# Front of a decoder block in two halves of the model width, with angles and three casts moved to GpSimd

## The chip, the cores and the metric

One core of a Trainium2 chip. The metric is the device time of one execution in microseconds (us). The kernel uses TensorE (PE; its weight loads are listed as PEld), VectorE (DVE), ScalarE (ACT), GpSimd (POOL) and SyncE (SP), which issues nearly all DMAs. Each engine runs its own list of instructions in order, and engines wait for each other on semaphores.

## The reference

x is 1024 tokens by a model width of 1024, one batch, one layer, all in float32:

```python
mod = (silu(c) @ w_ada + b_ada)          # 1024 -> 6 * 1024
sh1, sc1, g1, sh2, sc2, g2 = split(mod, 6)
h = rms_norm(x, norm1_g) * (1 + sc1) + sh1
q, k, v, u = split(h @ w_in)             # 512, 128, 128, 512 columns
q = rope(rms_norm(q, q_norm_g), cos, sin)       # cos, sin of positions * inv_freq
k = rope(rms_norm(k, k_norm_g), cos, sin)
attn = sliding_window_attention(q, k, v, sinks) # window 128, 8 heads on 2
pooled = trailing_means(u, (2, 4, 8, 16)) - u   # four groups of 128 channels
pool_out = (pooled @ pool_w) * pool_scale
x = x + g1 * (concat(attn, pool_out) @ w_o)
h2 = rms_norm(x, norm2_g) * (1 + sc2) + sh2
out = x + g2 * (square(relu(h2 @ w_mlp_in)) @ w_mlp_out)
```

The first rows of a trailing mean divide by the number of tokens there are (1, 2, ... up to the window).

## The kernel before, in words

**Precision.** Every operand of a projection is split in a high part (a cast to fp32r) and a low part (the float32 value less the high part). A product is three matmuls: high by high, low by high and high by low. The cast is ScalarE's work (names with `hi_`), the subtraction VectorE's (names with `lo_`).

**Tiles.** The tokens are eight tiles of 128 (t = 0 to 7). The model width is KD = 8 blocks of 128; NK = 4 is half of it.

**Modulation.** sh1 and sc1 are sums over the 1024 rows of w_ada. A row belongs to a partition and one of eight pieces, so VectorE multiplies a loaded piece (128 x 1024) by one column of silu(c) and adds it to an accumulator (`add_piece`, L1193 to L1199), eight pieces for sh1 in `acc`, then eight for sc1 in `acc_sc` (which is `squares`). PE then sums over the partitions with column sums: 128 columns of the accumulator as weights, a column of ones as the moving operand (`column_sum`, L2047). VectorE adds the biases and gains and has b1 (shift) and a1 (scale), one value for each of the 1024 columns of the width (L1251, `scale_1` at L1255).

**h.** x is loaded by tiles (`load_x`), squared and scaled by its root mean square (`square_x`, `root` on GpSimd, `scale_x`), turned by PE (`turn_x`) and multiplied by a1 and shifted by b1 as it is read from PSUM: the first half of the width by VectorE (`make_h`), the second by ScalarE (`make_h_half`). `hi_h` and `lo_h` split it. Both halves of a tile need all of a1 and b1 for their columns.

**Loads.** `stream` (L219) is the order in which SP loads the pieces: 8 of sh1, 8 of sc1, 4 of w_in for u (`wu`), 8 of w_in for q, k and v (`wqkv`), then the pieces of the later modulations, w_o, x and w1. Up to EARLY they go around twelve buffers (4 in `raw`, 8 in `slots`); a load waits for what was twelve places ahead to be used up (`freed`). x of tiles 0 and 1 goes behind the eighth piece (L540).

**The front on PE.** The order is written out by hand (L2177 to L2278): turn the bias and position rows; eight column sums of sh1; `turn_x(0)`, `turn_x(1)`; filler matmuls (`keep_clock`, which write nothing that is used) between the last pieces of sc1; column sums of sc1 in two halves; fillers; then tile 0's u projection over all eight blocks (`project_u_first`), its q, k and v (`project_qkv_first`), tile 1's u, `pool_windows(0)`, `turn_x(2)`, tile 1's q, `pool_out(0)`, tile 1's k and v, `turn_qk(0)`, tile 2's u. A column sum, a filler or any other matmul with float32 operands is two instructions in the trace, a transpose is one.

**Angles and sines.** VectorE computes positions times inverse frequencies and brings them into the range of the sine (`angles`, L1201), between `sum_qk(0)` and `norm_k(0)`. ScalarE takes the sines behind `scale_x(2)` (`sines`, L872).

**Pooling.** The trailing means are matmuls of u with four band matrices that GpSimd makes (`band`, L1853 to L1872). The first rows have other divisors, so GpSimd makes the bands for tile 0 first and rebuilds their first columns after tile 0's windows (L1927 to L1937).

**Later modulations.** sh2, sc2 and g1 are summed piece by piece in `acc`, one after the other, between the work of the tiles (`add_job_pieces`, with `first_pieces`, `between_pieces` and `late_pieces` giving the pieces of each tile, and JOB_LOADS the loads). Their sums are turned at t = 3 and t = 5.

Of the kernel before, what the change touches and what calls it, by code (L numbers as in the profile page):

```python
# [16 lines left out]
P = 128  # L17
# [36 lines left out]
def build(nc, x, c, positions, w_ada, b_ada, norm1_g, w_in, q_norm_g, k_norm_g, attn_sinks,  # L54
# [30 lines left out]
    with ExitStack() as ctx:  # L85
# [38 lines left out]
        mr = small[:, 90:98]  # L124

# [109 lines left out]
        JOB_LOADS = (4, 4, 4, 3, 4, 4, 1, 0)  # L235
        adaln_jobs = ("sh2", "sc2", "g1", "g2")
        mod_of = {"sh1": SH1, "sc1": SC1, "g1": G1, "sh2": SH2, "sc2": SC2, "g2": G2}
# [34 lines left out]
        a1_ready = sem("a1_ready")  # L272
        wu_hi, wu_lo = sem("wu_hi"), sem("wu_lo")
        wqkv_hi, wqkv_lo = sem("wqkv_hi"), sem("wqkv_lo")
# [55 lines left out]
        def xT_banks(t):  # L330
            return banks({0: 6, 1: 4, 2: 4}.get(t, 1))
# [148 lines left out]
        def freed(eng, n):  # L480

            before = buffer_of(n)[2]
            if before < 0:
                return
            kind, k = stream[before]
            if kind in ("sh1", "sc1"):

                eng.wait_ge(mod_summed, k + 1 + (KD if kind == "sc1" else 0) + (kind == "sc1" and k == KD - 1))
            elif kind in adaln_jobs:
                eng.wait_ge(job_summed, KD * adaln_jobs.index(kind) + k + 1)  # L490
            elif kind == "x":
                eng.wait_ge(x2_ready, k + 1)
            elif kind == "wo":
                wo_lo_made(eng, k)
            else:
                eng.wait_ge({"wu": wu_lo, "wqkv": wqkv_lo}[kind], k + 1)

        def source(kind, k):
# [8 lines left out]
            if kind == "w1":  # L507
                return w1[:, NK * (k % 2):NK * (k % 2) + NK, FB * (k // 2):FB * (k // 2) + FB]
            m = mod_of[kind]
            return wada[:, k, m * D:(m + 1) * D]  # L510

        def target(kind, a):
            if kind == "wu":
# [18 lines left out]
        def _(sp):  # L532
# [17 lines left out]
            load_x(2)  # L550
# [4 lines left out]
            sp.dma_start(sink, attn_sinks.to_broadcast([P, NH])).then_inc(params_in, 16)  # L555
            for t in range(NT):
                if 1 <= t and t + 2 < NT:
# [145 lines left out]
        def _(act):  # L703
# [20 lines left out]
            def make_h_half(t):  # L724

                if t == 0:
                    act.wait_ge(a1_ready, 2)
                act.wait_ge(x_turned, t + 1)
                for k in range(NK, KD):
                    ins = nc.scalar.activation(xh[:, t % 2, k * P:(k + 1) * P], xT_banks(t)[:, k * P:(k + 1) * P],  # L730
                                               ACT.Identity, bias=b1[:, k:k + 1], scale=a1[:, k:k + 1])
                ins.then_inc(h_half[1], 1)

            def hi_h(t, h):
                if t >= 3:
                    act.wait_ge(kv_done, t)
                elif t == 2:
                    act.wait_ge(kv_done, 1)
                act.wait_ge(h_half[h], t + 1)
                nc.scalar.copy(hT(t)[0][:, 4 * h:4 * h + 4, :], xh[:, t % 2, 512 * h:512 * h + 512]  # L740
                               .rearrange("p (k n) -> p k n", n=P)).then_inc(h_hi, 1)

            def hi_wu(j):
                a = landed(act, ("wu", j))
                nc.scalar.copy(wih[:, 2 * j:2 * j + 2, QKV:IN], a.rearrange("p (k n) -> p k n", k=2)).then_inc(wu_hi, 1)

            def hi_wqkv(k):
                a = landed(act, ("wqkv", k))
                nc.scalar.copy(wih[:, k, 0:QKV], a[:, 0:QKV]).then_inc(wqkv_hi, 1)

            square_x(0)
            square_x(1)
            scale_x(0)
            scale_x(1)
            hi_wu(0)
# [85 lines left out]
            def keep_u(t):  # L841
# [3 lines left out]
                nc.scalar.copy(usb[:, t % 2, :], bank(0)).then_inc(u_kept, 1)  # L845

            def square_q(t):
# [3 lines left out]
                nc.scalar.activation(squares[:, 0:AW], bank(6), ACT.Square).then_inc(q_squared, 1)  # L851

            def square_kv(t):
# [3 lines left out]
                nc.scalar.activation(squares[:, AW:AW + KVW], psum[:, 3, 0:KVW], ACT.Square).then_inc(kv_squared, 1)  # L857

            def hi_v(t):
                if t >= 4:  # L860
                    act.wait_ge(pv_done, 2 * (t - 2))
                nc.scalar.copy(vv[:, t % 4, :, 0, :],
                               psum[:, 3, KVW:2 * KVW].rearrange("p (g d) -> p g d", g=NKV)).then_inc(v_hi, 1)
# [15 lines left out]
            keep_u(0)  # L879
            hi_h(1, 0)  # L880
            hi_h(1, 1)
# [5 lines left out]
            sines()  # L887
            keep_u(1)
            keep_pooled(0)
# [3 lines left out]
            keep_pout(0)  # L893
            square_x(3)
            square_kv(1)
            hi_v(1)
            hi_qk(0)
            scale_x(3)
# [282 lines left out]
        def _(dve):  # L1181
# [19 lines left out]
            def angles():  # L1201
                a0, a1_, a2_ = (ang[:, j * ANG:(j + 1) * ANG] for j in range(3))
                a3 = ang[:, 3 * ANG:4 * ANG]
                inv = (np.float32(ROPE_THETA) ** (-np.arange(0, ROT_DIM, 2, dtype=np.float32) / np.float32(ROT_DIM)))
                for f in range(HALF):
                    ins = v.tensor_scalar(a0.rearrange("p (t f) -> p t f", f=HALF)[:, :, f], cols[:, 64:72],
                                          float(inv[f]), None, ALU.mult)
                own_d.step(ins)
                own_d.wait()
# [1352 lines left out]
```

## Time and profile before

| what | value |
|---|---|
| time, median of 3 runs | 939.24 us (938.83 to 939.59) |
| time of the profiled execution | 938.32 us |
| its span | 936.6 us |
| PE busy | 914.0 us (98% of the span) |
| weight loads busy | 764.0 us (82%) |
| VectorE, ScalarE, GpSimd busy | 647.6, 494.1, 359.1 us |
| HBM traffic | 187 GB/s over the span |

The span is what the profile shows of one execution, from its first to its last instruction; the execution's own time has 1.7 us more, which lie around it. All times in the rows are from the start of the span. In a view by time, a row is a start, a length, engine, line, operation and operands, "x" the number of instructions merged, and in brackets how long the engine had been idle and what released it.

### The profile page before, as it was taken

Reading aid. Unit: us, or ns where it says so; the run is one execution under the profiler, and the core shown is the slowest. Engines: PE = TensorE matmul, PEld = TensorE weight load, DVE = VectorE, ACT = ScalarE, POOL = GpSimd, SP = SyncE. Lnnn points to the kernel's source line nnn. Section 1 sums busy time; section 2 is a strip of 40 time slices with the busy share of each in tenths; the row PEclk is TensorE's granted clock in tenths of the full one; section 3 lists DMA queues with packets and bytes.
Section 4 is the critical chain, followed back from the end, with each engine's and each line's share of the span. In section 5 each row is a group of like instructions: output and inputs, shape, how many; then the busy total and the mean of one; then the engine's idle time right before and its main releaser. Section 6 shows DMA issues by size and latency. Waiting matters only on the chain.

```text
span 936.6 us, 12601 instructions
## 1 busy us (share of the span) xinstructions
PE 914.0 (98%) x4387; PEld 764.0 (82%) x4387; DVE 647.6 (69%) x999; ACT 494.1 (53%) x868; POOL 359.1 (38%) x346
## 2 busy tenths in 40 slices
PE   2999999999999999999999999999999999999998
PEld 2888888887888888888888878888888888888886
DVE  6988987877645778556554644445886566789896
ACT  2657888886655546654555444536434444333431
POOL 8272323233432447988888888721000000000000
PEclk9999999999999999999999999999999999999999
DMA  9953331235132413656544544359998538996772
GB/s 356 376 171 113 114 112 46 91 113 181 45 90 90 137 67 134 236 162 208 185 165 169 185 175 135 113 172 344 354 351 311 174 102 269 323 307 214 253 246 106
DMA packets 92271, 175.54 MB, mean 187 GB/s; under 512 B 9320, under 2 KB 26288, under 8 KB 92208
## 3 DMA queue, kind: packets, MB, share of 16 engines
q1 hardware_dynamic: 92096, 174.70, 55.3%
q8 instruction: 35, 0.57, 0.2%
q14 instruction: 28, 0.23, 0.1%
q10 hardware_dynamic: 112, 0.04, 0.0%
HBM read 136.95 MB, written 37.75 MB: 187 GB/s over the span
## 4 chain that ended last, share of the span: by engine, by line
PE 94%; DVE 3%; DMA 2%; SPq 1%; issue 0%; ACT 0%; DVEq 0%
PE psum L2034 27%; PE psum L2032 27%; PE psum L2033 27%; PE psum L2028 3%; DMA raw<-in_w_ada 2%; PE psum L2126 1%; PE psum L2127 1%; PE psum L2130 1%; PE psum L2112 1%; PE psum L2145 1%; DVE w_o_lo L1363 1%; PE psum L2172 1%; SPq L536 1%; PE psum L2202 1%; PE psum L2208 1%; PE psum L2205 0%
## 5 line engine op out<-in xcount | busy, mean ns | idle before, releaser
L1108 ACT CAST down_operands<-down_raw 128x1024 fp32r<-128x1024 f32 x96 | 100.8, 1053 | 152.7 <-PE psum L2034 62.6
L2032 PE MATMUL psum<-down_operands 128*128 128x512 f32 x448 | 174.3, 389 | 0.0
L2033 PE MATMUL psum<-down_operands 128*128 128x512 f32 x448 | 174.3, 389 | 0.0
L2034 PE MATMUL psum<-down_operands 128*128 128x512 f32 x448 | 174.3, 389 | 0.0
L1754 DVE TENSOR_TENSOR down_operands<-down_raw,down_operands 128x1024 fp32r<-128x1024 f32 x93 | 112.5, 1220 | 18.7 <-ACT down_operands L1108 18.1
L2032 PE MATMUL psum<-h2T,w_operands 128*128 128x512 f32 x272 | 106.7, 392 | 0.0
L2034 PE MATMUL psum<-h2T,w_operands 128*128 128x512 f32 x272 | 105.9, 389 | 0.0
L2033 PE MATMUL psum<-h2T,w_operands 128*128 128x512 f32 x272 | 105.8, 389 | 0.0
L2033 PEld LDWEIGHTS psum<-down_operands 128*128 128x128 f32 x448 | 84.1, 188 | 17.6
L2034 PEld LDWEIGHTS psum<-down_operands 128*128 128x128 f32 x448 | 84.1, 188 | 17.5
L2032 PEld LDWEIGHTS psum<-down_operands 128*128 128x128 f32 x448 | 84.1, 188 | 17.3
L1984 POOL TENSOR_TENSOR w_operands<-raw,w_operands 128x512 fp32r<-128x512 f32 x56 | 83.1, 1485 | 37.1 <-ACT w_operands L1060 37.1
L2034 PE MATMUL psum<-t_sums_hi,w_operands 128*128 128x512 f32 x168 | 65.4, 389 | 0.0
L2032 PE MATMUL psum<-t_sums_hi,w_operands 128*128 128x512 f32 x168 | 65.4, 389 | 0.0
L2033 PE MATMUL psum<-t_sums_lo,w_operands 128*128 128x512 f32 x168 | 65.4, 389 | 0.0
L2033 PEld LDWEIGHTS psum<-h2T,w_operands 128*128 128x128 f32 x272 | 51.1, 188 | 11.0 <-issue 0.5
L2032 PEld LDWEIGHTS psum<-h2T,w_operands 128*128 128x128 f32 x272 | 51.1, 188 | 11.0 <-issue 0.5
L1984 POOL TENSOR_TENSOR w_operands<-w_sums,w_operands 128x512 fp32r<-128x512 f32 x42 | 55.4, 1331 | 11.5 <-ACT w_operands L1060 11.5
L2034 PEld LDWEIGHTS psum<-h2T,w_operands 128*128 128x128 f32 x272 | 51.0, 188 | 10.6
L1060 ACT CAST w_operands<-w_sums 128x512 fp32r<-128x512 f32 x42 | 26.1, 623 | 55.9 <-PE psum L2034 53.3
L2032 PE MATMUL psum<-w_o_hi,mixT_hi 128*128 128x512 f32 x128 | 51.5, 403 | 0.0
L2034 PE MATMUL psum<-w_o_hi,mixT_lo 128*128 128x512 f32 x128 | 50.0, 391 | 0.0
(277 smaller groups left out, 1951.8 us busy)
## 6 DMA issues: line engine op xcount, KB each, us to landing
down_raw<-in_w_mlp_out SPq DMA_DIRECT2D x160, 256.0 KB, 4.3
down_raw<-act_scratch SPq DMA_DIRECT2D x112, 256.0 KB, 3.5
raw<-in_w_ada SPq DMA_DIRECT2D x32, 512.0 KB, 4.5
raw<-in_w_mlp_in SPq DMA_DIRECT2D x32, 512.0 KB, 5.0
act_scratch<-act_quads_a SPq DMA_DIRECT2D x64, 256.0 KB, 2.3
act_scratch<-act_quads_b SPq DMA_DIRECT2D x48, 256.0 KB, 3.6
slots<-in_w_ada SPq DMA_DIRECT2D x8, 512.0 KB, 10.6
xh<-in_x SPq DMA_DIRECT2D x8, 512.0 KB, 5.9
```

Source lines behind the costliest of these rows:

```text
L536: sp.dma_start(target(kind, piece_at(n)), source(kind, k)).then_inc(raw_in[buffer_of(n)[0]], 16)
L1060: nc.scalar.copy(w1op[:, w1_slot(b, name), 0, :, :], w1_quad(b, quad)).then_inc(w1_hi, 1)
L1108: nc.scalar.copy(o[:, 0, :, :], r[:, 0:2, :]).then_inc(op2_hi, 1)
L1363: v.tensor_tensor(wol[:, k, :], piece_at(place[("wo", k)]), woh[:, k, :].bitcast(F32), ALU.subtract).then_inc(wo_lo_dve, 1)
L1754: v.tensor_tensor(o[:, 1, :, :], r[:, 0:2, :], f32(o[:, 0, :, :]), ALU.subtract).then_inc(op2_lo_dve, 1)
L1984: g.tensor_tensor(o[:, 1, :, :], quad, o[:, 0, :, :].bitcast(F32), ALU.subtract).then_inc(w1_lo, 1)
L2028: return nc.tensor.transpose(o, i, ident[0:rows_, 0:rows_])
L2032: mm(o, wh, ah, start=first, stop=False, skip_group_check=adds)
L2033: mm(o, wh, al, start=False, stop=False, skip_group_check=adds)
L2034: return mm(o, wl, ah, start=False, stop=last, skip_group_check=adds)
L2112: ins = mm(o, qT[:, kv * G + h, :], k_, start=a == 0, stop=a == 1)
L2126: mm(bank(0), h[:, k, :], wih[:, k, QKV:IN], start=k == 0, stop=False)
```

## The change

1. **Halves.** A piece of the modulation (`mod`) now holds half of the width of sh1 and of sc1 (512 columns of each, two runs of 2 KB per partition). Eight pieces give b1 and a1 for blocks 0 to 3, eight more for blocks 4 to 7. `acc` holds the first half's sums, `acc_sc` the second's. The loads go: 8 mod, 2 wu, 4 wqkv, 8 mod, 4 wqkv, 2 wu; x of tiles 0 and 1 go behind the second piece.
2. **Accumulators.** Tiles 0 and 1 are projected over blocks 0 to 3 between the two halves of the modulation (`project_u_half`, `project_qkv_half`), and over blocks 4 to 7 behind it (`project_qkv_second` and the same). Tile 1 gets PSUM banks of its own: u in 1, q in 4, k and v in 5.
3. **h of tile 0.** Its second half is made by VectorE in two pairs of blocks (`make_h_front`), and ScalarE casts each pair (`hi_h_first`).
4. **GpSimd.** `angles` runs on GpSimd, 21 instructions. So do the casts of wu 1, wqkv 1 and wqkv 3. ScalarE's `sines` moves up ahead of hi_wqkv(4).
5. **Bands.** Tile 0's first columns get a small matrix of their own (`band_first`) and four more small matmuls; the rebuild goes.
6. **Later modulations.** sh2 and sc2 get accumulators of their own (in `slots`), no piece is added in tile 0 any more, and the sums are turned at t = 4 and 6.

The diff, cut to its core:

```diff
-        stream = [("sh1", k) for k in range(KD)]
-        stream += [("sc1", k) for k in range(KD)]
-        stream += [("wu", k) for k in range(KD // 2)]
-        stream += [("wqkv", k) for k in range(KD)]
+        stream = [("mod", k) for k in range(KD)]
+        stream += [("wu", 0), ("wu", 1)]
+        stream += [("wqkv", k) for k in range(NK)]
+        stream += [("mod", KD + k) for k in range(KD)]
+        stream += [("wqkv", k) for k in range(NK, KD)]
+        stream += [("wu", 2), ("wu", 3)]
...
-        JOB_LOADS = (4, 4, 4, 3, 4, 4, 1, 0)
+        JOB_LOADS = (4, 2, 3, 4, 4, 5, 2, 0)
...
+            if kind == "mod":
+                half = k // KD
+                return wada[:, k % KD, 0:2 * D].rearrange("p (m d) -> p m d", m=2)[:, :, 512 * half:512 * half + 512]
...
             def load_x(t):
                 if t >= 2:
-                    sp.wait_ge(h_lo, 2 * (t - 1))
+                    sp.wait_ge(h_lo, h_step(t - 2, 1))
...
-                if n == 7:
+                if n == 1:
                     load_x(0)
                     load_x(1)
...
```

ScalarE's order:

```diff
             square_x(0)
             square_x(1)
             scale_x(0)
             scale_x(1)
             hi_wu(0)
-            hi_wu(1)
-            hi_h(0, 0)
-            make_h_half(0)
-            hi_h(0, 1)
-            hi_wu(2)
-            hi_wu(3)
-            for k in range(5):
-                hi_wqkv(k)
-            make_h_half(1)
-            for k in range(5, KD):
-                hi_wqkv(k)
-            keep_u(0)
+            make_h_half(0, 0)
+            hi_h(0, 0)
+            hi_wqkv(0)
+            hi_wqkv(2)
+            make_h_half(1, 0)
             hi_h(1, 0)
+            sines()
+            hi_wqkv(4)
+            hi_wqkv(5)
+            hi_wqkv(6)
+            hi_h_first()
+            hi_wqkv(7)
+            hi_wu(2)
+            hi_wu(3)
+            make_h_half(1, 1)
             hi_h(1, 1)
             square_x(2)
             square_q(0)
             square_kv(0)
             hi_v(0)
             scale_x(2)
-            sines()
+            keep_u(0)
             keep_u(1)
...
```

VectorE's order:

```diff
+            sum_front(0)
+            shift_1(0)
             scale_1(0)
-            make_h(0, 0)
-            scale_1(1)
             lo_wu(0)
-            lo_h(0, 0)
             lo_wu(1)
+            lo_h(0, 0)
+            for k in range(NK):
+                lo_wqkv(k)
+            lo_h(1, 0)
+            sum_front(1)
+            lo_wqkv(4)
+            shift_1(1)
+            scale_1(1)
+            make_h_front()
+            lo_wqkv(5)
             lo_h(0, 1)
+            lo_wqkv(6)
+            lo_wqkv(7)
             lo_wu(2)
             lo_wu(3)
-            for k in range(KD - 1):
-                lo_wqkv(k)
-            make_h(1, 0)
-            lo_wqkv(KD - 1)
-            lo_h(1, 0)
             lo_h(1, 1)
...
             gain_q(0)
             sum_qk(0)
-            angles()
             norm_k(0)
...
```

GpSimd's order:

```diff
+            band_all(0)
+            pool.wait_ge(x_squared, 2)
+            root(rx[:, 0:2], ssx[:, 0:2], D, x_root)
+            band_all(1)
+            hi_wu_second()
+            hi_wqkv(1)
+            hi_wqkv(3)
+            angles()
+            band_all(2)
+            band_all(3)
...
```

TensorE's order:

```diff
+            tr(psum[:, 0, 0:72], rows[0:72, :], 72).then_inc(rows_turned, 1)
+            turn_x(0)
+            turn_x(1, 0, NK)
+            for n, fill in ((5, 3), (6, 5), (7, 3)):
+                pe.wait_ge(mod_summed, n)
+                keep_clock(fill, 3)
             pe.wait_ge(mod_summed, KD)
-            for k in range(KD):
-                ins = column_sum(psum[:, k // 4, k % 4:k % 4 + 1], acc, k)
+            for k in range(NK):
+                ins = column_sum(bank(1)[:, k:k + 1], acc, k)
             ins.then_inc(mod_turned, 1)
+            pe.wait_ge(mod_summed, KD + 1)
+            for k in range(NK):
+                ins = column_sum(bank(2)[:, k:k + 1], acc, NK + k)
+            ins.then_inc(sc1_turned, 1)
+            keep_clock(8, 3)
...
+            project_u_half(0, 0)
+            project_qkv_half(0, 0, (q_part(0), kv_part(0)))
+            project_u_half(1, 0)
+            project_qkv_half(1, 0, (q_part(1), kv_part(1)))
+            keep_clock(4, 2)
+            for n, fill in ((15, 4), (16, 3)):
                 pe.wait_ge(mod_summed, n)
                 keep_clock(fill, 2)
+            for m in range(2):
+                pe.wait_ge(mod_summed, 2 * KD + 1 + m)
+                for k in range(NK):
+                    ins = column_sum(bank(2)[:, NK * m + k:NK * m + k + 1], acc_sc, NK * m + k)
+            ins.then_inc(sc1_turned, 1)
+            pe.wait_ge(b1_second, 1)
+            pe.wait_ge(a1_ready, 2)
+            turn_x(1, NK, KD)
+            project_qkv_second()
+            project_u_half(0, 1)
+            project_u_half(1, 1)
+            pe.wait_ge(u_kept, 1)
+            turn_x(2)
+            project_qkv_half(1, 1, (q_part(1),))
             pool_windows(0)
+            project_qkv_half(1, 1, (kv_part(1),))
             pool_out(0)
             turn_qk(0)
             project_u(2)
...
```

`sum_front(0)` adds the eight pieces as before, the last in two halves of 512 columns; the positions are cast behind the fifth, and the columns copied behind the seventh. `angles` on GpSimd is eight products with the inverse frequencies, two instructions of rounding, three pairs of a product and a difference, and five more for the clamp, the absolute value and the shift by a quarter turn, each on 64 columns or fewer.

## Rows read from the trace of the kernel before

**Rows 1.** Busy time by window: PE, PEld, DVE, ACT, POOL, clock, DMA share, GB/s

```profile
20.00:32.00 12.00, 10.64 (x66) 10.07 (x66) 10.90 (x18) 4.41 (x6) 7.97 (x9) 1.00 1.04 398
...
90.00:105.00 15.00, 15.00 (x88) 13.08 (x87) 13.54 (x42) 12.84 (x35) 3.95 (x7) 1.00 0.43 134
```

**Rows 2.** PE's instructions by time: start us, us, instruction, times, idle before

```profile
20.76 3.68 PE L2028 MATMUL psum<-ident,xh 128*128 128x128 f32 x16 [0.98 <-ACT xh L721]
...
28.54 1.95 PE L2048 MATMUL psum<-ones,squares 128*128 128x1 f32 x16
...
32.10 1.20 PE L2202 MATMUL psum<-w_in_hi,hT_hi 128*128 128x512 f32 x4 [0.62 <-ACT hT_hi L740]
...
46.46 0.39 PE L2126 MATMUL psum<-w_in_hi,hT_second 128*128 128x512 f32 x1
...
51.93 1.14 PE L2172 MATMUL psum<-band,u_rows 128*128 128x144 f32 x8
52.91 1.04 PE L2028 MATMUL psum<-ident,xh 128*128 128x128 f32 x8
53.70 0.47 PE L2032 MATMUL psum<-w_in_hi,hT_second 128*128 128x512 f32 x1
...
59.27 1.05 PE L2145 MATMUL psum<-pooledT,pool_w 128*128 128x128 f32 x8
60.08 0.36 PE L2032 MATMUL psum<-w_in_hi,hT_second 128*128 128x256 f32 x1
...
63.03 0.81 PE L2028 MATMUL psum<-ident,qkn 128*128 128x128 f32 x6
63.61 0.47 PE L2126 MATMUL psum<-w_in_hi,hT_hi 128*128 128x512 f32 x1
```

**Rows 3.** VectorE by time, in the front

```profile
18.19 0.75 DVE L1196 TENSOR_SCALAR squares<-slots,small 128x1024 f32<-128x1024 f32 x1 [1.90 <-DMA slots<-in_w_ada]
19.46 3.93 DVE L1198 SCALAR_TENSOR_TENSOR squares<-slots,small,squares 128x1024 f32<-128x1024 f32 x3 [0.52 <-DMA slots<-in_w_ada]
...
27.73 1.42 DVE L1238 SCALAR_TENSOR_TENSOR squares<-raw,small,squares 128x512 f32<-128x512 f32 x2
...
30.02 1.37 DVE L1272 TENSOR_SCALAR xh<-psum,small 128x128 f32<-128x128 f32 x4
...
31.57 1.23 DVE L1285 TENSOR_TENSOR w_in_lo<-slots,w_in_hi 128x1024 fp32r<-128x1024 f32 x1
32.72 0.68 DVE L1278 TENSOR_TENSOR hT_lo<-xh,hT_hi 128x512 fp32r<-128x512 f32 x1
...
37.43 0.95 DVE L1291 TENSOR_TENSOR w_in_lo<-slots,w_in_hi 128x768 fp32r<-128x768 f32 x1
```

**Rows 4.** ScalarE by time, at the end of the front

```profile
28.90 1.04 ACT L745 CAST w_in_hi<-slots 128x1024 fp32r<-128x1024 f32 x1 [7.16 <-DMA slots<-in_w_in]
30.25 1.04 ACT L745 CAST w_in_hi<-slots 128x1024 fp32r<-128x1024 f32 x1 [0.31 <-DMA slots<-in_w_in]
31.42 0.62 ACT L740 CAST hT_hi<-xh 128x512 fp32r<-128x512 f32 x1
31.95 1.50 ACT L730 ACTIVATE xh<-psum,small 128x128 f32<-128x128 f32 x4
...
35.91 0.83 ACT L749 CAST w_in_hi<-slots 128x768 fp32r<-128x768 f32 x1
```

**Rows 5.** Column sums: weight loads, ns min/median/max, first and last start

```profile
L2048 PEld LDWEIGHTS psum<-ones,acc x16: 288/333/337, 16.2 to 19.4; 128*128 128x128 f32 x16
...
L2048 PEld LDWEIGHTS psum<-ones,squares x16: 186/192/192, 28.5 to 30.2; 128*128 128x128 f32 x16
```

**Rows 6.** GpSimd's groups by shape: busy us, mean ns, idle before

```profile
L1892 POOL CAST w_o_hi<-raw 128x1024 fp32r<-128x1024 f32 x1 | 1.0, 1037 | 5.9 <-PE psum L2034 5.9
```

**Rows 7.** GpSimd by time: VectorE idle at 3.8, adding at 26.5

```profile
3.82 0.29 POOL L1837 TENSOR_SCALAR_AFFINE_SELECT band<-band 128x128 f32<-128x128 f32 x1
...
26.49 1.25 POOL L1870 COPY small<-small 128x1 f32<-128x1 f32 x1
```

More of the change, by code:

```diff
@@ new lines, in band_all, with hi_wu_second, hi_wqkv @@
+            def band_all(i):
+                band_of(i, band[:, i, 0:P], 0)
+                band_of(i, band[:, i, P:BAND], P)
+                own_p.step(less_token(i, P))
+            def hi_wu_second():
+                a = landed(pool, ("wu", 1))
+                g.tensor_copy(wih[:, 2:4, QKV:IN], a.rearrange("p (k n) -> p k n", k=2)).then_inc(wu_hi[1], 1)
+            def hi_wqkv(k):
+                a = landed(pool, ("wqkv", k))
+                g.tensor_copy(wih[:, k, 0:QKV], a[:, 0:QKV]).then_inc(wqkv_hi[1], 1)
@@ L1926, in _ @@
                 g.tensor_tensor(part[:, :, 1, :], rot[:, 1, :, 0, :], rot[:, 1, :, 1, :], ALU.add).then_inc(qk_roped, 1)
-                if t == 0:
-                    pool.wait_ge(band_done, 1)
-                    for i, w in enumerate(POOL_WINDOWS):
-                        own_p.step(g.memset(band[:, i, 0:w], 1.0 / w))
-                        own_p.wait()
-                        band_of(i, band[:, i, 0:w], 0)
-                        if i + 1 < NP:
-                            own_p.step(less_token(i, w))
-                            own_p.wait()
-                    less_token(NP - 1, POOL_WINDOWS[-1]).then_inc(consts_made, 1)
             def root_x2(i):
@@ L2034, in three, with turn_x @@
                 return mm(o, wl, ah, start=False, stop=last, skip_group_check=adds)
-            def turn_x(t):
+            def turn_x(t, first=0, end=KD):
                 pe.wait_ge(x_scaled, t + 1)
-                for k in range(KD):
-                    ins = tr(xT_banks(t)[:, k * P:(k + 1) * P], xh[:, t % 2, k * P:(k + 1) * P])
+                for k in range(first, end):
+                    ins = tr(xT_block(t, k), xh[:, t % 2, k * P:(k + 1) * P])
                 ins.then_inc(x_turned, 1)
@@ new lines, in lo_hi, with hi_lo, project_u_half @@
+            def lo_hi(o, t, k, a, b):
+                return mm(o, hT(t)[1][:, k, :], wih[:, k, a:b], start=False, stop=False)
+            def hi_lo(o, t, k, a, b):
+                return mm(o, hT(t)[0][:, k, :], wil[:, k, a:b], start=False, stop=k == KD - 1)
+            def project_u_half(t, half):
+                o, ks = u_bank(t), range(NK * half, NK * half + NK)
+                pe.wait_ge(h_hi, h_step(t, half))
+                if (t, half) == (0, 0):
+                    pe.wait_ge(cols_ready, 1)
+                elif (t, half) == (1, 0):
+                    pe.wait_ge(mod_taken, 1)
+                for k in ks:
+                    hi_made(pe, wu_hi, k // 2)
+                    hi_hi(o, t, k, QKV, IN)
+                pe.wait_ge(wu_lo, 2 * half + 1)
+                if half == 0:
+                    for k in ks[0:2]:
+                        hi_lo(o, t, k, QKV, IN)
+                pe.wait_ge(h_lo, h_step(t, half))
+                for k in ks:
+                    lo_hi(o, t, k, QKV, IN)
+                if half == 1:
+                    for k in ks[0:2]:
+                        hi_lo(o, t, k, QKV, IN)
+                pe.wait_ge(wu_lo, 2 * half + 2)
+                for k in ks[2:4]:
+                    ins = hi_lo(o, t, k, QKV, IN)
+                if half == 1:
+                    ins.then_inc(u_done, 1)
@@ new lines, in project_qkv_half @@
+            def project_qkv_half(t, half, parts):
+                pe.wait_ge(h_hi, h_step(t, half))
+                for k in range(NK * half, NK * half + NK):
+                    hi_made(pe, wqkv_hi, k)
+                    for o, a, b, _ in parts:
+                        hi_hi(o, t, k, a, b)
+                    pe.wait_ge(h_lo, h_step(t, half))
+                    for o, a, b, _ in parts:
+                        lo_hi(o, t, k, a, b)
+                    pe.wait_ge(wqkv_lo, k + 1)
+                    for o, a, b, done in parts:
+                        ins = hi_lo(o, t, k, a, b)
+                        if k == KD - 1:
+                            ins.then_inc(done, 1)
```

413 lines of the change are left out of this document (201 added, 212 removed).

## The prediction

> **What bounds the kernel now.** I read the profile in the order page, windows, PE's instructions by time, then VectorE, ScalarE and GpSimd beside them. The page has PE busy for 98% of the span. The windows say where the rest is: from 20 to 32 us PE is busy, but with fillers, transposes and column sums; from 90 to 105 it is busy without a gap [rows 1]. So the kernel is a front, in which PE has no weights and no h to work on, and then a run in which PE sets the time. Only the front can give anything, and what it gives is kept as long as the next stages stay PE's. The front ends at 32.10 us with the first real projection, and PE starts tile 2's u projection at 63.61 [rows 2]. I compare that second mark, since both kernels have done the same work by then.
>
> What holds the front is the modulation: VectorE adds 16 pieces at 1.31 us (3.93 for 3), which is nearly the pace at which they land (the weights behind them come at 28.90 and 30.25, 1.35 apart) [rows 3, 4].
>
> **What moves ahead.** A tile's projection is 5.47 us for u (46.46 to 51.93), 5.57 for q (53.70 to 59.27) and 2.95 for k and v (60.08 to 63.03), 13.99 in all [rows 2]. Half of it for two tiles is 14.0 us of PE work that now runs while the second half of the modulation is loaded and added. What is left behind the second half, from its first matmul S to tile 2's u, is the other 14.0, and turn_x(2) 0.79, pool windows 0.98, pool_out 0.81 and turn_qk 0.58 [rows 2]. The windows of tile 0 gain four small matmuls for the first positions, two instructions each; at a column sum's 0.12 (1.95 for 16) that is about 0.9. Together 18.1 us. The change breaks even at S = 63.6 - 18.1 = **45.5 us**. Before, that work began at 32.1 and was all in one piece; the question is how much later than 32.1 the second half begins.
>
> **The first half of the modulation.** Same bytes, in 2 KB rows, as the w_in pieces for u have; at their 1.35 us, behind x0 and x1, the eighth piece lands at about 5.3 + 9 x 1.35 = 17.4, and VectorE ends it at 19.2 to 19.6. PE can't start before the positions are cast, behind the fifth piece (about 15.0). Then it has 12 transposes of x at 0.22 (3.68 for 16 in the cold front), to 18.3, and then the 11 filler calls, 22 instructions, that stand in its queue ahead of the column sums. Their three waits have passed by then, so all of them run in front. PE's weight loads take 333 ns at this point of the kernel before and 192 later [rows 5], with the granted clock given as full (2.4 GHz) in both; I take half pace for part of them, 3.6 us, to 21.9. Sixteen column sums at 0.12 end at 23.9, and a1 and b1 of the first half stand at **24.2**. With the fillers at full pace it is 23.2; with all at half pace, 25.1.
>
> **VectorE from there.** ScalarE makes h and casts it (1.50 + 0.62 [rows 4]), so PE starts at 26.3. VectorE has lo_wu twice (1.23 each), lo_h (0.68), lo_wqkv four times (0.9 each) and lo_h [rows 3]: 7.3 us. One of the GpSimd casts (1.04 for 1024 columns [rows 6], so some 0.8 for 768) falls between two of them and holds VectorE for 0.8; the other two lie where VectorE waits. The second sum starts at 32.3. All its pieces but the last have landed by then or land on time, so it is VectorE's own: 0.75 + 6 x 1.31 + 1.42 = 10.05 us, to **42.35**.
>
> PE meanwhile does its 14.0 us, with 0.3 of waiting for the low part of h, to 40.6; then 11 filler calls at 0.11 per instruction, 2.4 us, to 43.0: later than the sums, so they cost 0.7. Column sums to 44.95, scale and shift to 45.3, the first two blocks of h 0.7 (half of 1.37), their cast 0.35: S would be **46.5**, 1.0 late already.
>
> **The angles.** This is the step that I think decides. VectorE did them behind tile 0's q, beside PE work. Now they are 21 instructions of GpSimd, tiny ones, and ScalarE's queue has the sines ahead of hi_wqkv(4), (5) and (6); VectorE in turn has lo_wqkv(4) ahead of shift_1(1) and scale_1(1). So a late angle holds the whole second half. GpSimd's price for a tiny instruction is in the trace: a 128x128 select takes 0.29 us while VectorE is idle, but a copy of a single column takes 1.25 us beside VectorE's two-input adds [rows 7]. It ends when the add ends; in the front every GpSimd instruction that reads does so, one to each VectorE instruction (about ten such rows), while memsets aren't held. The angles start at about 26. Until 42.35 VectorE has 16 instructions that hold it, so 16 of the 21 are done; the other five then run free at about 0.27, by the select's price, to 43.7. Sines 0.7, hi_wqkv(4) 0.75 [rows 4], lo_wqkv(4) 0.95, shift and scale 0.5, two blocks 0.7, cast 0.35: **S = 47.7**, 1.2 us more. The bounds: nothing, if two or more GpSimd instructions slip into each gap; 5 us more, if GpSimd gets no gap and all 21 run free from 42.35 on.
>
> The rows of the adds show their pitch unchanged at 1.31 beside GpSimd. The Trainium skill (SBUF — State Buffer, "Who interferes with whom") says that a VectorE instruction with two SBUF inputs and a GpSimd instruction that reads SBUF take one port pair in turn, each for its whole length. By that rule taken to the letter the adds would also be held by 0.2 for each angle, and the sum would be 1.6 us more; I go by the rows.
>
> **Behind S.** hi_wqkv(7) and lo_h(0,1) stand behind the work above, for 0.5 us of waits in the second half of q, k and v. x of tile 2 is loaded only after lo_h(0,1), and ScalarE has its square, three more instructions and the scaling ahead of keep_u(0): about 0.4. Tile 2's u starts at 47.7 + 18.1 + 0.9 = 66.7, **3.1 us later** than before. The three band matrices and consts_made have 10 us before pool_windows(0) asks for them: nothing. In the later tiles three pieces (3.9 us) are added to VectorE's load in all, over five tiles in which it is busy 13.54 of 15 us; PE covers that [rows 1]: 0, at most 1, and not below 0, since PE has no idle there to give back. Tile 0's second band rebuild on GpSimd goes; nobody waited for it.
>
> **The sum.** The profiled execution took 938.32 us, 0.9 under the median. 938.3 + 3.1 = 941.4 on its own scale, and **942.3** against the median of 939.24.
>
> **Rivals.**
> - *VectorE keeps up with the loads* (faster). The second modulation has landed by 34.9. If a1 came at 21 and neither the low parts nor GpSimd's casts held the second sum, it would end near 37.6, S would be near 41, and tile 2's u near 59: 4 to 5 us gained, about 935. For it: VectorE idles some 4 us before a1, and PE's first work is off the path. Against it: its queue is a fixed order of two-input work, which I can only shorten by an earlier a1. It decides below S = 43.6. Chance 0.20.
> - *The angles are in time.* GpSimd gets more than one instruction into a gap, or ScalarE isn't held. Then S = 46.5 or a little less, tile 2's u starts at about 64.8, and the time is 940.3, inside what can be told apart. Chance 0.25.
> - *PE's clock falls.* From 43.0 to 47.7 PE has column sums, four transposes and idle time. The longest gap in the front before, behind the fillers, is 0.62 us [rows 2], and there is nothing of this length in the trace. If PE starts the second half at its lower level (1.2 GHz), some 5 us of it take twice as long, as in the front before: 2.5 us more, 944.8. The Trainium skill (TensorE: Matmul & The Clock Gate, "What's actually happening") says that an idle PE is set to half rate and gets the full one back after sustained work; no row here has it fall. Chance 0.15.
> - *The forecast*: 0.40.
>
> **How the numbers follow.** A measurement of this kernel can tell about 0.2% (1.9 us) from no change. Slower by more takes the forecast and the clock, 0.55; same takes the second rival, 0.25; faster takes the first, 0.20. The likeliest case alone is 941 to 944. The range goes up over the clock and a part of the upper bound of the angles, to 947, and down into the first rival, to 936, leaving out its better half.
>
> **What would show it.** Right: GpSimd's tiny instructions at 0.9 to 1.3 us from 26 to 42; ScalarE idle for over 10 us ahead of the sines; the last piece summed at about 42; S at about 47.7 and tile 2's u at about 66.7. Wrong: angles ready before 41; a1 before 23; S before 45. It would also be wrong if the time moved behind tile 2, where I expect nothing.

## The result, and the profile after

The changed kernel takes **942.93 us** (median of 6 runs, 942.36 to 943.82) against 939.04 (938.41 to 939.59) of the kernel before, in runs side by side: a ratio of 1.0043, 95% interval 1.0033 to 1.0053. It is 3.9 us slower, 0.4%; the forecast was 942.3. The profiled execution took 942.73, 4.4 us more than that of the kernel before (938.32).

The page of the kernel after, head and busy times:

```profile
span 941.0 us, 12655 instructions
## 1 busy us (share of the span) xinstructions
PE 916.3 (97%) x4421; PEld 766.8 (81%) x4421; DVE 642.3 (68%) x976; ACT 494.4 (53%) x874; POOL 370.3 (39%) x341
```

PE is still busy for 97%. Its instructions by time in the front (start us, us, instruction, times, idle before), which answer to [rows 2]:

```profile
15.84 0.35 PE L2097 MATMUL psum<-ident,probs 72*128 72x72 f32 x1 [15.84 <-DVE probs L1265]
15.98 2.77 PE L2097 MATMUL psum<-ident,xh 128*128 128x128 f32 x12
18.54 3.42 PE L2114 MATMUL psum<-ident 128*128 128x128 f32 x22
21.79 1.84 PE L2117 MATMUL psum<-ones,acc 128*128 128x1 f32 x16
...
26.28 1.20 PE L2276 MATMUL psum<-w_in_hi,hT_hi 128*128 128x512 f32 x4 [0.75 <-ACT hT_hi L779]
...
40.28 2.62 PE L2114 MATMUL psum<-ident 128*128 128x128 f32 x22
42.74 1.84 PE L2117 MATMUL psum<-ones,squares 128*128 128x1 f32 x16
46.76 0.63 PE L2097 MATMUL psum<-ident,xh 128*128 128x128 f32 x4 [2.18 <-DVE small L1279]
47.97 2.93 PE L2276 MATMUL psum<-w_in_hi,hT_hi 128*128 128x512 f32 x8 [0.58 <-ACT hT_hi L786]
...
59.09 1.03 PE L2097 MATMUL psum<-ident,xh 128*128 128x128 f32 x8
...
66.85 0.82 PE L2097 MATMUL psum<-ident,qkn 128*128 128x128 f32 x6
67.42 0.47 PE L2198 MATMUL psum<-w_in_hi,hT_hi 128*128 128x512 f32 x1
```

The mark of the prediction, tile 2's u, stands at 67.42 instead of 63.61: 3.8 us late. S, the first matmul of the second half, is the row at 47.97. Ahead of it PE has a wait of 2.18 us for b1 of the second half. VectorE and ScalarE by time tell why b1 is late:

```profile
31.54 0.74 DVE L1244 TENSOR_SCALAR squares<-raw,small 128x1024 f32<-128x1024 f32 x1
...
33.64 6.57 DVE L1246 SCALAR_TENSOR_TENSOR squares<-slots,small,squares 128x1024 f32<-128x1024 f32 x5
40.24 1.42 DVE L1261 SCALAR_TENSOR_TENSOR squares<-slots,small,squares 128x512 f32<-128x512 f32 x2
45.36 0.96 DVE L1326 TENSOR_TENSOR w_in_lo<-slots,w_in_hi 128x768 fp32r<-128x768 f32 x1 [3.70 <-ACT w_in_hi L795]
```

```profile
43.84 0.69 ACT L905 ACTIVATE trig<-probs 128x64 f32<-128x64 f32 x4 [12.79 <-POOL probs L1915]
44.45 1.55 ACT L795 CAST w_in_hi<-slots 128x768 fp32r<-128x768 f32 x2
```

VectorE ends the second sum at 41.66, and then idles 3.70 us for hi_wqkv(4), which stands on ScalarE behind the sines, which wait 12.79 us for the angles. GpSimd by time:

```profile
25.84 6.51 POOL L1894 TENSOR_SCALAR probs<-cols 128x8 f32<-128x8 f32 x8
32.43 1.28 POOL L1898 TENSOR_SCALAR probs<-probs 128x64 f32<-128x64 f32 x1
...
43.57 0.24 POOL L1915 TENSOR_SCALAR probs<-probs 128x64 f32<-128x64 f32 x1
...
48.15 6.14 POOL L1949 TENSOR_TENSOR small<-small,ident 128x16 f32<-128x16 f32 x1
```

The first rows are the angles, 0.81 us for an instruction on eight columns and 1.28 on 64. The last was a surprise (below). And PE, behind S, runs at its lower level; by window (us, PE busy, clock, DMA share, GB/s):

```profile
47.00:48.00 1.00, 0.42 (x5) 0.75 0.00 0
48.00:49.00 1.00, 1.00 (x3) 0.50 0.00 0
49.00:50.00 1.00, 1.00 (x4) 0.50 0.00 0
50.00:51.00 1.00, 1.00 (x5) 0.54 0.43 49
51.00:52.00 1.00, 1.00 (x7) 1.00 0.85 315
```

From about 47.5 to 50.9 the granted clock is 0.5, that is 1.2 GHz: the eight matmuls at S (four of 512 columns, four of 256, merged in one row) take 2.93 us, and the same eight 2.00 at full clock (first and third experiments).

### The profile page after: what moved, and what is told of

Its sections match the earlier page's. It is cut to its first block, busy times and chain, and to the rows that moved or that the text cites. A ratio compares the mean times of both kernels' runs of the same rounds, so it can differ in the third digit from the quotient of the medians.

```text
span 941.0 us, 12655 instructions
## 1 busy us (share of the span) xinstructions
PE 916.3 (97%) x4421; PEld 766.8 (81%) x4421; DVE 642.3 (68%) x976; ACT 494.4 (53%) x874; POOL 370.3 (39%) x341
## 4 chain that ended last, share of the span: by engine, by line
PE 90%; DVE 3%; POOL 2%; DMA 2%; ACT 1%; issue 1%; SPq 0%; DVEq 0%
PE psum L2103 26%; PE psum L2102 26%; PE psum L2101 26%; PE psum L2097 3%; DMA raw<-in_w_in 1%; PE psum L2182 1%; DMA raw<-in_w_ada 1%; PE psum L2198 1%; PE psum L2199 1%; PE psum L2202 1%; DVE w_o_lo L1404 1%; PE psum L2276 1%; POOL probs L1894 1%; PE psum L2218 1%; DVE probs L1369 1%
```

## The experiments

Three theories. **A**: the angles are late, and as ScalarE's queue has the sines ahead of hi_wqkv(4), they hold S. **B**: GpSimd's angles hold VectorE's sums. **C**: the fall of the clock is part of the loss. A fourth came out of the first runs, **D**: S earlier is worth as much as S moves, break-even S near 45. "Kernel 5" is the kernel of experiment 5. Experiments 1 to 4, 5 to 8 and 9 to 11 were each run together with the kernel before, whose medians were 938.95, 938.34 and 939.16 us. Across these groups compare the ratios and the traces, not the times; the ratios are over all runs and not quite those of the medians. No experiment takes the three casts, the bands or the later modulations apart, so their share in the 3.9 us isn't measured.

**1. Sines moved behind scale_x(2) (A).**

```diff
             hi_h(1, 0)
-            sines()
...
             scale_x(2)
+            sines()
             keep_u(0)
```

> The changed kernel with one line moved: ScalarE takes the sines behind scale_x(2) again; the angles stay on GpSimd. Theory A (late angles hold ScalarE's queue, and through hi_wqkv(4) and lo_wqkv(4) the second half): lo_wqkv(4) runs at about 41.7 us instead of 45.4, the first matmul of the second half starts at about 46.6 instead of 47.97, the angles themselves are ready as late as before (about 43.8), and the time is 1.3 us less, about 941.6; about 940.2 if the clock, which fell to half at 47.5 in the changed kernel, then holds too. Theory B (VectorE's and PE's own chain sets the second half, the angles lie beside it): start unchanged within 0.3, time 942.9.

Measured: 941.14 us, ratio 1.0027 (1.0018 to 1.0037); one of its ten runs took 945.08, the others 940.99 to 941.32. PE by time:

```profile
44.90 0.63 PE L2097 MATMUL psum<-ident,xh 128*128 128x128 f32 x4 [0.57 <-DVE small L1279]
46.11 2.00 PE L2276 MATMUL psum<-w_in_hi,hT_hi 128*128 128x512 f32 x8 [0.58 <-ACT hT_hi L786]
...
57.35 1.09 PE L2097 MATMUL psum<-ident,xh 128*128 128x128 f32 x8 [0.95 <-ACT u_rows L874]
```

The wait for b1 falls from 2.18 to 0.57, S goes from 47.97 to 46.11, the clock holds. The angles are ready at 44.0, as late as before, and now nobody asks. A holds. Of the 1.9 us at S, tile 2's u keeps 1.7 (65.75): the fall of the clock went as well, but a new wait of 0.95 for keep_u(0) takes most of that. On ScalarE keep_u(0) now stands behind the sines I moved, which take 1.9 us there, 1.28 of it for the load of their table.

**2. Angles back on VectorE, behind the sum of q and k; sines as in 1 (B).**

```diff
             sum_qk(0)
+            angles()
```

> The changed kernel with the angles undone altogether: on VectorE behind sum_qk(0), sines behind scale_x(2). Theory A: as the run with the sines late, 941.6 or 940.2, within 0.4 us of it: it was the place in ScalarE's queue that cost, not GpSimd's work beside VectorE. If GpSimd's small instructions also held VectorE's sums back (port taken in turn), the second sum (10.1 us in the changed kernel) gets shorter by up to 1.6 and the time falls by as much again. If the angles are worth moving at all, this kernel is slower than the one with the sines late, by up to 2.8 us.

Measured: 941.96 us, ratio 1.0033 (1.0020 to 1.0045). The five whole adds of the second sum take 6.65 us together, and 6.57 in the kernel after. GpSimd isn't idle beside them (the bands have moved into the angles' place, to 39.4), but it is beside the last piece: its two halves take 1.42 us here, and 1.42 in the kernel after with angles beside them. B falls. S is at 46.27. The time is 0.8 us above that of 1, where I had expected 0.4 at most, since the sines now wait 1.45 us for VectorE, ahead of keep_u(0): turn_x(2) waits 2.11.

**3. The kernel after, with 12 filler calls ahead of turn_x(1) (C).**

```diff
             ins.then_inc(sc1_turned, 1)
+            keep_warm(12)
             pe.wait_ge(b1_second, 1)
```

> The changed kernel with 12 filler calls (24 instructions, 2.6 us) on PE between the second half's column sums and the second part of turn_x(1). Theory C (the fall of the clock costs what the slow matmuls lose, about 2.9 us of PE work at half pace, less the 0.5 us that it would have waited anyway): the granted clock stays full from 47 to 51 us, the first matmul stays at 48.0, and the time is 1.0 to 1.5 us less, about 941.7. Rival: PE waits for weights and the low part of h there anyway, the fall costs nothing: 942.9. Fillers that run too long would push the start by up to 0.4.

Measured: 941.58 us, ratio 1.0029 (1.0018 to 1.0040). The clock is full in every window from 44 to 53.

```profile
47.93 2.00 PE L2281 MATMUL psum<-w_in_hi,hT_hi 128*128 128x512 f32 x8
...
58.07 1.03 PE L2097 MATMUL psum<-ident,xh 128*128 128x128 f32 x8
```

S stands where it was (47.93) and turn_x(2) comes 1.0 us earlier. The fall costs 1.0 us, and 1.35 by the medians, which are of two groups of runs. C holds.

**4. The kernel before, with its angles on GpSimd behind consts_made.**

```diff
             sum_qk(0)
-            angles()
...
+            angles()    # on GpSimd, behind consts_made
```

> The kernel before with one part of the change alone: the angles on GpSimd (behind consts_made, from about 28.6 us), the sines where they were. Price of the angles by theory A: one instruction to each two-input instruction of VectorE, 0.9 us here instead of 1.3, so the 21 take about 15 us and are ready near 44 to 46, before the sines are asked for at 51; PE covers VectorE's 2.8 us there, so the time is 939.0, within 0.4. Rival: VectorE's work between 49 and 52 us was on the path, and the kernel gets 0.5 to 1.5 us faster.

Measured: 938.76 us, ratio 0.9997 (0.9988 to 1.0007). GpSimd needs 14 us for them (28.25 to 42.4), and it costs nothing, since the sines are far behind, at 51.37. So with this order of the queues it is the place of the sines that costs, not the engine of the angles; kernels 8 and 10 will show the engine at a price too.

**5. Kernel 1, with 2 filler calls instead of 11 ahead of the second column sums (D).**

```diff
-            keep_clock(4, 2)
-            for n, fill in ((15, 4), (16, 3)):
-                pe.wait_ge(mod_summed, n)
-                keep_clock(fill, 2)
+            keep_clock(2, 2)
```

> The run with the sines late, and of the 11 filler calls ahead of the second half's column sums only two left. Theory D (those fillers stand in PE's queue behind its 14 us of work and hold the column sums: 42.5 us, where the sums are ready at 40.6 and 41.3): column sums run from about 40.6 to 42.4, the first matmul of the second half starts at 44.2 instead of 46.1, time 1.9 us less, about 939.2. Rival (without them the clock falls as in the changed kernel): granted clock at half for some us after the start, which gives back 1 to 1.5 us, 940.5.

Measured: 941.44 us, ratio 1.0027 (1.0016 to 1.0039): no gain over 1, where I had expected 1.9 us. S moves as D says, to 44.17. PE by window, then PE and GpSimd by time:

```profile
44.00:45.00 1.00, 0.83 (x3) 0.50 0.00 0
45.00:46.00 1.00, 1.00 (x4) 0.50 0.00 0
```

```profile
57.74 1.09 PE L2097 MATMUL psum<-ident,xh 128*128 128x128 f32 x8 [2.46 <-ACT u_rows L874]
```

```profile
53.47 0.56 POOL L1887 TENSOR_TENSOR small<-small 128x1 f32<-128x1 f32 x1
```

The clock falls, and turn_x(2) waits 2.46 for keep_u(0) instead of 0.95. The wait is longer than what the fall costs, so the fall is hidden in it. What holds keep_u(0) is GpSimd's root for x of tile 2: it ends at 54.03, and at 53.63 in 1, though S is 1.9 earlier; scale_x(2) waits 2.53 for it, and turn_x(2) comes 0.4 later than in 1, as the root does. In 1, where the fillers stand in this place, the clock held.

**6. Kernel 1, with the positions cast behind the second piece, and 7 instead of 11 filler calls in front.**

```diff
-                    if half == 0 and k == 4:
+                    if half == 0 and k == 1:
...
-            for n, fill in ((5, 3), (6, 5), (7, 3)):
+            for n, fill in ((5, 3), (6, 2), (7, 2)):
```

> The run with the sines late, the positions cast behind the second piece instead of the fifth (so PE turns x from about 14.5 us instead of 15.2) and 7 filler calls instead of 11 ahead of the first column sums. Theory E (a1 stands at 23.7 because of PE's queue of transposes and fillers, not because of the sums, ready at 19.5): column sums from about 20.3, a1 at about 22.7, the start of the second half 0.9 to 1.1 us earlier (45.1), time about 940.1. Rival: with fewer fillers PE's pace rises later, column sums take 3.6 us instead of 1.8 and a1 stays where it was: 941.1.

Measured: 943.58 us, ratio 1.0044 (1.0031 to 1.0058); of its seven runs one was at 940.01, the others from 942.06 to 943.90. S is at 43.55, 4.4 us earlier than in the kernel after, the clock holds up to there, and the kernel is no faster. GpSimd and then PE by time, and PE by window:

```profile
43.57 6.27 POOL L1873 TENSOR_SCALAR_AFFINE_SELECT band<-band 128x16 f32<-128x16 f32 x1
...
53.71 0.19 POOL L1885 TENSOR_SCALAR small<-small 128x1 f32<-128x1 f32 x1
```

```profile
58.26 1.21 PE L2097 MATMUL psum<-ident,xh 128*128 128x128 f32 x8 [4.43 <-ACT u_rows L874]
```

```profile
57.00:58.00 1.00, 0.00 (x0) 1.00 1.01 406
...
60.00:61.00 1.00, 1.00 (x4) 0.50 0.00 0
```

One select of 16 columns takes 6.27 us. It starts with VectorE's run of seven two-input low parts (43.61 to 49.78) and ends with it. Behind it in GpSimd's queue are the bands, consts_made and, at 53.71, the root for x of tile 2. scale_x(2) waits 3.91 for that, and then the sines and keep_u(0) follow on ScalarE: PE idles 4.43 us, and behind this wait its granted clock is 0.5, from 59.1 to 62.5. This is the next bound of the front, and I had put it down as nothing.

**7. Kernels 5 and 6 together, and lo_wu(0) ahead of shift_1(0).**

> Both of these together, and lo_wu(0) ahead of shift_1(0) in VectorE's queue, where it idles for 3 us. By the prediction's first rival (VectorE keeps up with the loads) this is what it takes: second sum ended at about 40 instead of 41.3, first matmul of the second half at about 42.7, tile 2's u about 62.3 against 63.6 in the kernel before, time about 937.7, the first one faster than the kernel before. If PE's own 14 us of the first halves set it (end 39.1), nothing more comes from VectorE and it is 938.2.

Measured: 944.84 us, ratio 1.0063 (1.0048 to 1.0078). S at 43.03, the clock down from 43 to 47, turn_x(2) at 58.64 behind a wait of 4.13. Behind this wait the clock falls a second time, from 56.9 to 63.7. I had expected 937.7. Three ways to make S earlier, and the slowest kernel of the study: what comes ahead of S is not the bound any more.

**8. Kernel 7, with keep_u(0) ahead of scale_x(2) and the sines last.**

```diff
-            scale_x(2)
-            sines()
             keep_u(0)
+            scale_x(2)
             keep_u(1)
+            sines()
```

> The run before it, with keep_u(0) ahead of scale_x(2) and the sines behind keep_u(1) on ScalarE. turn_x(2) waited 0.95 us for keep_u(0) in the run with the sines late. Theory: that wait goes, 0.6 to 0.9 us less than the run before it, about 937.0. Rival: x of tile 2 (loaded only behind the low part of tile 0's h) is the later one, and the wait passes to the scaling: no change.

Measured: 939.79 us, ratio 1.0005 (0.9995 to 1.0015), where I had expected 937.0. Three of its ten runs took 937.78 to 938.40, the others 939.14 to 940.12; the profile is of one of the others (939.89), so what the three had isn't shown. GpSimd, then PE:

```profile
43.02 6.27 POOL L1915 TENSOR_SCALAR probs<-probs 128x64 f32<-128x64 f32 x1
...
54.02 0.19 POOL L1885 TENSOR_SCALAR small<-small 128x1 f32<-128x1 f32 x1
```

```profile
56.19 1.07 PE L2097 MATMUL psum<-ident,xh 128*128 128x128 f32 x8 [1.75 <-ACT xh L755]
```

Same S (42.95), 5 us faster than 7: turn_x(2) comes 2.45 earlier, and the rest is the second fall of the clock, which is gone. What is left is a wait of 1.75 for scale_x(2) itself, and so for GpSimd's root at 54.02. Here it is the last angle that is held for 6.27.

The last three were run together (before: 939.16).

**9. Kernel 8, with the angles back on VectorE and 5 filler calls ahead of turn_x(1).**

> The kernel of e8 with the angles back on VectorE (behind the sum of q and k of stretch 0) and five filler calls between the last column sums and turn_x(1). Theory D (the bound behind S is now GpSimd's queue up to root_x(2), and the clock): with the angles gone from GpSimd, root_x(2) ends near 50.5 instead of 54.5, turn_x(2) loses its wait of 1.75 us, and the fillers keep the clock at full rate, worth 1.0 to 1.5 us (e3 against the kernel after): turning of q and k near 61.5 and 936.0 to 937.0 us, under both kernels. Rival F (VectorE's 2.8 us of angles stand ahead of norm_k of stretch 0, as in the kernel before): the turning of q and k is late by about as much as was gained, 938.5 to 939.5. Rival G (what is gained in front is given back behind it, at the next tiles' modulation): the turning is early, and the time stays within 0.5 us of e8's 939.8.

**10. The same without the 5 filler calls.**

> As e9 without the five filler calls. Theory D: root_x(2) near 50.5, no wait of turn_x(2), the clock falls as in e8: turning of q and k near 62.3 and 937.5 to 938.3 us. Rival F: no change against e8, 939 to 940. Against e9 it prices the clock alone: 1.0 to 1.5 us dearer.

**11. Kernel 8, with the root for x of tile 2 ahead of the bands of tiles 2 and 3.**

```diff
             angles()
+            pool.wait_ge(x_squared, 3)
+            root(rx[:, 2:3], ssx[:, 2:3], D, x_root)
             band_all(2)
...
-                if t == 0:
-                    root_x(2)
```

> The kernel of e8 with root_x(2) ahead of the bands of tiles 2 and 3 on GpSimd, the angles staying there. Theory D: root_x(2) follows x_squared(2) or the held angle instruction, whichever is later, near 50.5 to 51.5, so turn_x(2) waits for at most 0.3 us instead of 1.75, and the time is 1.3 to 1.7 us under e8's, about 938.2 us. Rival H (the angle instruction that is held for 6 us ends only near 49.3 and later ones are held too): root_x(2) past 53 and no change. If D is right, the bands' place in the queue was the price, not the angles as such.

Measured: kernel 9 takes **937.72 us**, ratio 0.9984 (0.9974 to 0.9993); kernel 10 938.25, 0.9988 (0.9979 to 0.9998); kernel 11 939.91, 1.0006 (0.9997 to 1.0016). PE of kernel 9:

```profile
24.23 2.06 PE L2279 MATMUL psum<-w_in_hi,hT_hi 128*128 128x512 f32 x4 [2.04 <-ACT hT_hi L779]
...
42.00 1.36 PE L2117 MATMUL psum<-ident 128*128 128x128 f32 x10
43.20 0.60 PE L2095 MATMUL psum<-ident,xh 128*128 128x128 f32 x4
43.92 2.00 PE L2279 MATMUL psum<-w_in_hi,hT_hi 128*128 128x512 f32 x8
...
54.04 1.03 PE L2095 MATMUL psum<-ident,xh 128*128 128x128 f32 x8
...
62.37 0.47 PE L2201 MATMUL psum<-w_in_hi,hT_hi 128*128 128x512 f32 x1
```

Not a wait from the second column sums to tile 2's u. GpSimd does the root at 50.33; the clock is full from 42 to 64; tile 2's u starts at 62.37, 1.24 ahead of the kernel before, and the times agree (1.4 by the medians, 1.0 between the profiled executions). The gain is 0.16%, small, but the interval leaves out zero. Its median misses my 936 to 937 by 0.7. The first row shows what may be left in it: behind a wait of 2.04 us the clock is down from 24.3 to 27.7 (in kernel 10 too), these four matmuls take 2.06 us where kernel 8 has 1.19, and the second column sums start 1.1 us later than in kernel 8. No run has more fillers in that place. In kernel 10 S is at 43.96, but the clock is down from 44.8 to 48.2, and tile 2's u is at 63.72: 1.35 later by the traces, but 0.5 by the medians, less than the 1.0 to 1.5 I had expected. The profiled execution of kernel 10 (939.04) is the second slowest of its ten runs, so the pair of traces shows more than the difference of the kernels. Kernels 8 and 10 differ in the angles' engine alone, and the ratio goes from 1.0005 to 0.9988, some 1.6 us; the two intervals just touch. Rival F, VectorE's angles ahead of norm_k(0), didn't come: they lie from 52.16 to 55.0, for the most part beside GpSimd's root for q and k (to 54.6), which norm_k(0) needs anyway.

Kernel 11 is a miss of mine. The wait at turn_x(2) goes, as D says (53.28, no wait), but another takes its place. VectorE, then PE, then ScalarE:

```profile
57.48 0.61 DVE L1451 SCALAR_TENSOR_TENSOR qkn<-psum,small,gqk 128x128 f32<-128x128 f32 x2 [5.30 <-POOL small L1887]
```

```profile
62.19 1.13 PE L2218 MATMUL psum<-pooledT,pool_w 128*128 128x128 f32 x8 [1.89 <-issue]
```

```profile
59.98 1.14 ACT L779 CAST hT_hi<-xh 128x512 fp32r<-128x512 f32 x2 [2.52 <-DVE xh L1307]
...
61.52 0.57 ACT L898 COPY pooledT<-psum 128x512 f32<-128x512 f32 x1
```

The bands now stand ahead of the root for q and k of tile 0, which ends at 57.4. norm_k(0) waits 5.30 for it, and PE gets a stall of 1.89 further down, at pool_out(0). The trace names no releaser for it, but ScalarE's rows and the order of the queues give the chain: VectorE makes tile 2's h behind norm_k(0) (58.20 to 59.56), ScalarE waits 2.52 for it, and keep_pooled(0), which pool_out(0) needs, stands behind that cast and ends at 62.09. That fits, and no run takes it apart. Tile 2's u is 0.8 earlier than in 8 in the profiled execution, in which the clock held, and by the medians there is no gain. The 4.6 us of bands and constants behind one held instruction are in the way of one root or of the other; in kernel 9 they are done by 39.5.

## Why the prediction was right, and where its steps were off

The time (942.3 against 942.93) and the mechanism were right: a second half that starts too late, held by the angles through ScalarE's queue. The sum was a little short: 3.1 us of change against 3.9 by the medians and 4.4 between the profiled executions (941.4 against 942.73 on their scale). The 1.3 us between 3.1 and 4.4 are 0.3 at S, 0.4 behind it and 0.6 in the later tiles. The steps can be laid beside the trace.

- **First half.** a1 was forecast at 24.2 and stands at 24.0; fillers 3.6 us against 3.42; PE's start 26.3 against 26.28.
- **Second sum.** Forecast from 32.3 to 42.35, measured from 31.54 to 41.66: its length (10.05 against 10.12) was right, its start was forecast 0.8 too late. VectorE's work up to there takes 7.6 us (from 23.95) and not 8.1: lo_wu twice takes 2.99 with GpSimd's cast beside it, some 0.5 more than 2 x 1.23, where I had the cast cost 0.8.
- **PE to the column sums.** 43.0 and 44.95 against 42.74 and 44.6.
- **Angles.** Ready at 43.7 forecast, 43.8 measured. One to each VectorE instruction holds: the first eight take 0.81 each, beside eight VectorE instructions of 0.7 to 1.2, those from 32 to 40 take 1.0 to 1.4 beside the adds, the next two, beside the halves of the last piece, 0.62 and 0.65, and the last ones ran free. So the sign "0.9 to 1.3 us from 26 to 42" fits only roughly. S at 47.7 against 47.97, and experiment 1 gives the price of the queue: 1.9 us at S where I had 1.2, because without it the column sums end at 44.3 and S would be 46.1, not 46.5. (The terms of the 46.5 add up to 46.35.)
- **The adds beside GpSimd.** Their pitch stayed at 1.31. The Trainium skill (SBUF — State Buffer, "Who interferes with whom") would have them held by each angle. The halves of the last piece (1.42 with GpSimd at work and without, experiment 2) disagree, and going by the rows gave the right length. It isn't nothing everywhere, though: in experiment 1 seven GpSimd instructions got in between VectorE's low parts, and that run took 6.5 us instead of 6.2.
- **Behind S.** Forecast 18.1 of work and 0.9 of waits. Kernel 9, with no wait and a full clock, shows the work: 62.37 - 43.92 = 18.45, so the break-even S is 45.2 and not 45.5. In the kernel after it is 19.45, and the other 1.0 isn't the waits, which the trace doesn't show (turn_x(2) has none), but the clock. So my term of 0.9 had the right size by luck, for the wrong reason: **the rival of the falling clock came true beside the forecast**, at 1.0 us and not 2.5. I had taken the length of the low stretch (about 5 us) from the cold front; it was 3.4 us, and the matmuls in it didn't take twice as long: the eight at S take 2.93 us instead of 2.00, the next eight, which start near its end, 1.68 instead of 1.57. In experiment 6, where the fall meets nothing but matmuls of 512 columns, one takes 0.43 us from start to start instead of 0.23. The two were never exclusive, and my chances treated them so.
- **Bands and consts: "nothing".** True in the kernel after, where the root for x of tile 2 came at 54.79 and PE didn't wait. But it was true by 2 us only; experiments 6 to 8 ran into it at once.
- **Later tiles.** Forecast 0, at most 1. From tile 2's u to the head of the MLP another 0.6 is lost (3.8, then 4.4 late), inside the bound, though any move behind tile 2 was to be a sign of being wrong. Part of it is two waits that the kernel before doesn't have, 0.24 at pool_out(1) and one at turn_x(4):

```profile
PE psum L2097 <- DVE kT L1399: 0.4, 1, 0.4
```

The rival on the other side (VectorE keeps up with the loads, S near 41) was not only late by VectorE's order. Its condition was "below S = 43.6"; experiments 6 and 7 reached 43.55 and 43.03 and were slower than the kernel before. The step that failed there is the one that took what lies behind S as fixed. Even kernel 9 gains 1.4 us at S = 43.9, in a front of 62.

## What to carry to other kernels

When an early start has been bought, look at every queue that must now deliver earlier, not only at the one that was late: here the second half could move 4 us ahead and gain nothing, until keep_u, the root and the angles had been put in the order in which PE asks for them. A step that nobody waits for belongs behind everything that somebody waits for on its queue; on which engine it is done matters where its queue holds something else that is waited for, as in kernel 8 against 10. And filler matmuls that look like waste at the end of a stretch may be what keeps the clock: take them out only with the windows of the clock beside you.

## What I had not expected of the hardware

- **A small GpSimd instruction held for 6 us.** It occurred in the kernel after (6.14) and in experiments 3 (6.15), 6, 7, 8 and 11 (6.27 each), each time on an instruction of at most 64 columns that started within 0.11 us of the start of VectorE's run of seven two-input instructions, and each time it ended with that run. I had priced it as held to the end of one. In experiments 1 and 5 the same run let one through in nearly every gap; in 1:

```profile
48.91 0.92 POOL L1946 TENSOR_SCALAR_AFFINE_SELECT small<-small 128x16 f32<-128x16 f32 x1
49.91 1.07 POOL L1949 TENSOR_TENSOR small<-small,ident 128x16 f32<-128x16 f32 x1
```

  In these two the first GpSimd instruction beside the run started 0.25 us after the run's start. Whether that decides is open; no run here took it apart.
- **The clock after a quiet stretch.** Ahead of the fall PE had done column sums and four transposes, with 2.8 us of idle time in the kernel after, and 1.0 to 1.4 in experiments 5, 7 and 8 and kernel 10. In experiments 1, 2, 6 and 11, with 1.1 to 1.2, it held. Where it falls can't be told from these rows; that five filler calls ahead of S held it in the profiled execution of kernel 9 can.
- **The kernel before isn't free of it.** I took its clock as steady, from one profile. In the profile of experiment 4, whose TensorE order is that of the kernel before, the clock is down from 30.6 to 34.0, and the first four matmuls take 2.08 us instead of 1.20. The 68 runs of the kernel before beside the experiments fit: the 24 with a mean granted clock of 1.000 took 938.04 to 938.59 us, the others 938.34 to 940.90. That is about 1 us of scatter in the reference, as much as some of the differences read above. Kernel 9's gain stands even so: its four runs at 1.000 took 936.74 to 937.78 us, and the eight of the kernel before beside them 938.13 to 938.59.
